# State-space branch: a quarter's circle computed behind the copy of the linear that ends next

## Chip, cores and metric

One core of one Trainium2 chip runs the whole program. The metric is the device time of one execution in microseconds (us); the kernel before takes 3046.33 us, the median of 3 runs (3044.68 to 3046.96).

## What is computed

Two transformer-like blocks on 512 tokens of width 1024, in float32. The change lies in the first block, in its state-space (S5) branch, which runs interleaved with the linears of the block's other branches:

```python
def first_block(x, ...):
    n = rms_norm(x, mix_norm_g)
    proj = n @ w_in
    xa, zu, zv = proj[..., :OFF_U], proj[..., OFF_U:OFF_V], proj[..., OFF_V:OFF_GA]
    gate_a, gate_b = sigmoid(...), sigmoid(...)
    ya = s5_branch(xa, ...)        # this one
    yb = sgu_branch(zu, zv, ...)
    ...

def s5_scan(u, lam_re, lam_im, log_step, b_re, b_im, c_re, c_im, reverse):
    lam_bar = exp(lam * step)
    b_bar = ((lam_bar - 1.0) / lam)[..., None] * b
    bu = einsum('gpc,lbgc->lbgp', b_bar, u)
    _, states = associative_scan(_linear_recurrence, (a, bu), axis=0, reverse=reverse)
    return einsum('gcp,lbgp->lbgc', c, states).real
```

The states are complex. The kernel takes 8 tokens as one chunk, so that 64 chunks are scanned, and rotates the inputs of the scan by the angle of each chunk, scans real and imaginary parts with a real decay, and rotates back. The cosines and sines of these angles are "the circle".

## The kernel before

Every linear is cut into units of 128 rows of its weight matrix (8 units for most linears). For each unit SyncE loads the weights into one of 8 slots, ScalarE rounds them to `wH` (`round_units`, L1321, an ACTIVATE Copy of 128x512), GpSimd subtracts to get the rest `wL` (L2874), and TensorE does 12 matmuls (L726: three passes over four blocks). `wH` and `wL` have four buffers, so ScalarE rounds a unit once the unit four before it has been used up.

PSUM is two halves of four banks. Half 0 takes the linears of this stretch (`azv0`, `azv1`, `azu0`, `azu1`, `aga0`, `agb0`), half 1 takes the small jobs of the state-space branch. When a linear ends, `linear_read` (on ScalarE, L1334) reads its four banks one by one with Gelu or Sigmoid; the next linear's first unit writes bank by bank behind it. A job of half 1 waits, in `fill`, until the job before it in the half has been read (`drained[1]`).

The order is written out by hand in `S5_STEPS`, a list of (task, quarter, units of the linears done before it), which TensorE and ScalarE both follow. The branch runs in four quarters. Those steps that matter, with the units: `("taps", 1, 14), ("turn_y", 0, 16), ("drive", 1, 17)`, then `("taps", 2, 23), ("turn_y", 1, 24), ("drive", 2, 25)` and `("taps", 3, 31), ("turn_y", 2, 32), ("drive", 3, 33)`. So on TensorE the order is: taps of quarter q (L866), one or two units, `turn_y` of quarter q-1 (32 small transposes, L906), one unit, `drive` of quarter q (64 small matmuls, L880), further units. Units 15, 23 and 31 (counted from 0) are the last of `azv1`, `azu0` and `azu1`.

On ScalarE each step first rounds the units that are due (four ahead of TensorE), with `linear_read` ahead of the rounding that pairs with a linear's last unit, and then does the step's task: for `turn_y` the copy `turned_y` of the transposed outputs from half 1 (an ACTIVATE Copy, L1312, which also frees half 1), for `out` a Gelu from PSUM (L1312) and the rounding of the next quarter's angles (L1469), for `taps` of quarters 1 to 3 `circle(q)`: Abs (L1474), Sin (L1475) and Sin (L1476), each 128x512, the Abs and the first Sin each waited for by the next. Sin and Gelu need different activation tables, and the compiler puts an ACT_TABLE_LOAD where the table changes.

VectorE rounds off the angles (`fraction`, L2224), which `circle(q)` waits for, and its `scan(q)` (L2318 and on) waits for `drive(q)` and for the circle. `out(q)` on TensorE waits for the states of `scan(q)`.

Of the kernel before, what the change touches and what calls it, by code (L numbers as in the profile page):

```python
# [57 lines left out]
SPLITS = 4  # L58
# [248 lines left out]
def two_blocks(nc, I, out):  # L307
    ring, jobs = Ring(), Jobs()
    ds = bass.ds
    with ExitStack() as ctx:  # L310
# [161 lines left out]

        forward = [[(0, 512, 0, 0)], [(1, 384, 512, 512), (3, 128, 896, 896)], [(2, 256, 1024, 1024)]]
        ret_at = {j: to for bank in forward for j, _, _, to in bank}

        def done(eng, name, l=0, i=0):
# [19 lines left out]
        def read_out(eng, name, l=0, i=0):  # L496

            eng.wait_ge(drained[jobs.half[name]], jobs.nth(name, l, i) + 1)
# [808 lines left out]
        def _(act):  # L1307
            link = Chain(act, S["act_step"])
            act.dma_start(consts[:, 0:2 * P], I["consts"][:, 0:2 * P]).then_inc(S["consts_loaded"], 16)
            def evac(dst, src, h, func=ACT.Copy, **kw):  # L1310

                act.activation(dst, src, func, **kw).then_inc(drained[h], 1)  # L1312

            def round_units(name, l, i, units, cols):
                for u in units:
                    s, p = ring.slot[(name, u)], ring.split[(name, u)]
                    act.wait_ge(landed[s], ring.at(ring.landed, name, u, l, i))
                    free = ring.at(ring.before, name, u, l, i) + ring.split_room[(name, u)]
                    if free > 0:
                        act.wait_ge(weights_used, free)  # L1320
                    act.activation(wH[:, p, 0:cols], slot[:, s, 0:cols], ACT.Copy).then_inc(weights_high, 1)  # L1321
# [135 lines left out]
            def plain_x(g):  # L1457

                act.wait_ge(S["plain_turned"], g + 1)
                h = jobs.half["aplain1" if g else "ahx0"]  # L1460
                evac(hT[:, 4 * g:4 * g + 4, :], banks(h), h)
# [4 lines left out]
            def angles_whole(q):  # L1466

                act.wait_ge(S["s5_angles"], 2 * q + 1)
                act.activation(decays_k, rot_cos, ACT.Identity, bias=rounder).then_inc(S["s5_circles"], 1)  # L1469

            def circle(q):

                act.wait_ge(S["s5_angles"], 2 * q + 2)
                link(act.activation(decays_k, rot_sin, ACT.Abs))  # L1474
                link(act.activation(rot_sin, rot_sin, ACT.Sin, scale=-TWO_PI))  # L1475
                act.activation(rot_cos, decays_k, ACT.Sin, bias=half_pi, scale=-TWO_PI).then_inc(S["s5_circles"], 1)  # L1476
# [8 lines left out]
            def turned_y(q):  # L1485

                act.wait_ge(S["s5_y_turned"], q + 1)
                evac(y[:, q, :].rearrange("p (k s) -> p s k", s=8), ps[1][:, 0:T].rearrange("p (s k) -> p s k", s=8), 1)

            def linear_read(name):  # L1490

                done(act, name)
                h = jobs.half[name]
                if name == "azv0":
                    act.wait_ge(S["x_moved"], 16)
                if name[:3] == "azv":
                    at = 512 * int(name[3])
                    evac_by_bank(zv[:, :, at:at + 512], h, ACT.Gelu_apprx_tanh)
                elif name[:3] == "azu":
                    at = 4 * int(name[3])  # L1500
                    evac_by_bank(zu[:, at:at + 4, :], h, ACT.Gelu_apprx_tanh)
                else:
                    evac_by_bank(gates_a[name[1:]], h, ACT.Sigmoid)

            ahead_units = S5_UNITS + [("aglu", u) for u in range(4)]
            rounded = SPLITS
            for task, q, units in S5_STEPS:
                for (name, u), (used, of_it) in zip(ahead_units[rounded:units + SPLITS], S5_UNITS[rounded - SPLITS:units]):
                    if of_it == KD - 1:
                        linear_read(used)  # L1510
                    round_units(name, 0, 0, [u], 512)
                rounded = units + SPLITS
                if task == "plain":
                    plain_x(q)
                elif task == "turn_u":
                    act.wait_ge(S["s5_u_turned"], 1)
                    evac(ush, ps[1][:, :].rearrange("p (g k) -> p g k", k=CHUNKS), 1)
                elif task == "turn_v":
                    act.wait_ge(S["s5_v_turned"], q + 1)
                    evac(VT, ps[1][:, :].rearrange("p (n e s) -> p n e s", n=2, e=8), 1)  # L1520
                elif task == "taps" and q:
                    circle(q)
                elif task == "out":
                    act.wait_ge(S["s5_out"], q + 1)
                    evac(yk.rearrange("p s (j c) -> p j s c", j=4), ps[1][:, 0:T].rearrange("p (j s c) -> p j s c", j=4, s=8), 1,
                         ACT.Gelu_apprx_tanh)
                    if q < QUARTERS - 1:
                        angles_whole(q + 1)
                    if q == 2:
                        act.dma_start(wsn, I["sgu_w"].rearrange("h t s -> t h s")).then_inc(S["sgu_w_loaded"], 16)  # L1530
                    elif q == 3:
                        act.dma_start(lng, I["sgu_ln_g"].unsqueeze(0).to_broadcast([P, D])).then_inc(S["sgu_loaded"], 16)
                        act.dma_start(lnb, I["sgu_ln_b"].unsqueeze(0).to_broadcast([P, D])).then_inc(S["sgu_loaded"], 16)
                        act.dma_start(sgub, I["sgu_bias"].unsqueeze(0).to_broadcast([P, H, P])).then_inc(S["sgu_loaded"], 16)
                elif task == "turn_y":
                    turned_y(q)
                    if q == 2:
                        read_out(act, "aturn_y2")
                        act.activation(yH[:, 0:3, :], y[:, 0:3, :], ACT.Copy).then_inc(S["ya_high"], 1)
                    elif q == 3:  # L1540
                        read_out(act, "aturn_y3")
                        act.activation(yH[:, 3, :], y[:, 3, :], ACT.Copy).then_inc(S["ya_high"], 1)
                if task == "drive" and q == 3:
                    act.wait_ge(S["zv_moments"], 1)
                    act.activation(stat[:, 56:60], stat[:, 48:56].rearrange("p (a b) -> p a b", b=2)[:, :, 1], ACT.Sqrt, bias=eps)\
                       .then_inc(S["zv_moments"], 1)
# [1426 lines left out]
```

## Time and profile before

| what | value |
|---|---|
| median of 3 runs | 3046.33 us |
| the profiled execution: time | 3046.19 us |
| the profiled execution: span, first to last instruction | 3044.4 us |
| TensorE busy | 3000.9 us, 99% of the span |
| ScalarE busy | 1279.4 us, 42% |
| VectorE busy | 1377.9 us, 45% |
| GpSimd busy | 1390.1 us, 46% |
| mean granted TensorE clock | 0.997 |

The profile is of one execution. A line names an engine (PE is TensorE, DVE VectorE, ACT ScalarE, POOL GpSimd), the line of the kernel, the operation and its tiles. Instructions of an engine overlap at their ends, so the time between two starts, not the duration, is what a further one adds. TensorE's granted clock is 1.00 at 2.4 GHz and 0.50 at 1.2 GHz.

### The profile page before, as it was taken

What the parts mean: (1) busy time and instruction counts of PE and PEld (TensorE: products, weight loads), DVE (VectorE), ACT (ScalarE), POOL (GpSimd) and SP (SyncE); (2) the same over time, 40 slices, a digit from 0 to 9 for tenths busy, and PEclk for the clock granted to TensorE, in tenths of its full rate; (3) what the DMA queues carried; (4) which work ended last, traced back from release to release, by engine and by line L of the source; (5) the groups of instructions that cost most, each with busy time, mean ns of one, the idle gap of its engine ahead of it and who ended that gap; (6) DMA issues with size and microseconds to landing.
All of it is one profiled execution on the core that took longest, in us unless ns stands there. A gap on an engine that the chain in (4) does not pass through costs nothing.

```text
span 3044.4 us, 39864 instructions
## 1 busy us (share of the span) xinstructions
PE 3000.9 (99%) x15302; PEld 2426.5 (80%) x15302; DVE 1377.9 (45%) x2171; ACT 1279.4 (42%) x2203; POOL 1390.1 (46%) x1002
## 2 busy tenths in 40 slices
PE   8999999999999999999999999999999999999998
PEld 7778887788888777778888888878777788878887
DVE  7874351421114877562116433167866520264322
ACT  5443343433333445454234443244454433354432
POOL 6335574444444542134455454554322354544543
PEclk9999999999999999999999999999999999999999
DMA  5334242233333422123333333244231133333332
GB/s 158 85 110 144 87 135 87 80 97 97 99 96 92 135 76 81 49 67 87 97 92 99 94 97 98 84 111 136 71 86 41 61 101 97 97 91 97 97 97 72
DMA packets 214891, 287.61 MB, mean 94 GB/s; under 512 B 42682, under 2 KB 122610, under 8 KB 213042
## 3 DMA queue, kind: packets, MB, share of 16 engines
q1 hardware_dynamic: 212210, 279.88, 31.5%
q0 software_dynamic: 880, 2.99, 0.3%
q8 instruction: 121, 1.98, 0.3%
q10 hardware_dynamic: 1616, 2.23, 0.2%
q14 instruction: 64, 0.52, 0.1%
HBM read 269.80 MB, written 4.72 MB: 90 GB/s over the span
## 4 chain that ended last, share of the span: by engine, by line
PE 91%; DVE 4%; ACT 2%; POOL 1%; issue 1%; DMA 0%; SPq 0%; ACTq 0%; DVEq 0%
PE half L726 81%; PE half L1125 2%; PE half L1156 2%; PE half L1142 2%; PE half L1211 1%; POOL wL L2874 1%; DVE arena L2052 1%; PE half L981 0%; PE half L998 0%; DVE rms L2043 0%; PE half L1197 0%; PE half L896 0%; DVE nL L2059 0%; ACT arena L1334 0%; DMA slot<-in_w_in 0%
## 5 line engine op out<-in xcount | busy, mean ns | idle before, releaser
L2874 POOL TENSOR_TENSOR wL<-slot,wH 128x512 fp32r<-128x512 f32 (+1 forms) x976 | 1358.4, 1399 | 1624.8 <-ACT wH L1321 1623.7
L1321 ACT ACTIVATE wH<-slot 128x512 fp32r<-128x512 f32 (+1 forms) x976 | 603.7, 625 | 1228.7 <-PE half L726 1223.5
L726 PE MATMUL half<-nH,wH 128*128 128x512 f32 x2336 | 924.1, 396 | 8.8 <-POOL wL L2874 3.2
L726 PE MATMUL half<-nH,wL 128*128 128x512 f32 x2336 | 910.5, 390 | 0.0
L726 PE MATMUL half<-nL,wH 128*128 128x512 f32 x2336 | 909.4, 389 | 0.0
L726 PE MATMUL half<-arena_split,wH 128*128 128x512 f32 (+1 forms) x2432 | 735.8, 385 | 2.6 <-ACT arena L1334 1.4
L726 PEld LDWEIGHTS half<-nH,wH 128*128 128x128 f32 x2336 | 438.4, 188 | 118.6 <-issue 18.1
L726 PEld LDWEIGHTS half<-arena_split,wH 128*128 128x128 f32 x2432 | 451.1, 188 | 95.4 <-issue 4.2
L726 PEld LDWEIGHTS half<-nH,wL 128*128 128x128 f32 x2336 | 438.5, 188 | 92.4
L726 PEld LDWEIGHTS half<-nL,wH 128*128 128x128 f32 x2336 | 438.8, 188 | 89.3 <-issue 1.4
L726 PE MATMUL half<-arena_split,wL 128*128 128x512 f32 (+1 forms) x1216 | 466.4, 384 | 0.0
L726 PEld LDWEIGHTS half<-arena_split,wL 128*128 128x128 f32 x1216 | 228.5, 188 | 45.2
L2790 DVE TENSOR_TENSOR arena<-half,arena 128x2048 f32<-128x2048 f32 x16 | 36.7, 2292 | 322.6 <-PE half L726 306.8
L2822 DVE SCALAR_TENSOR_TENSOR arena<-half,vec,arena 128x511 f32<-128x511 f32 (+1 forms) x160 | 108.8, 743 | 159.7 <-ACT arena L1984 159.0
L1833 ACT ACTIVATE arena<-half 128x512 f32<-128x512 f32 (+2 forms) x128 | 68.5, 535 | 230.5 <-PE half L1142 230.5
L2073 DVE TENSOR_TENSOR arena_split<-arena,arena_split 128x1024 fp32r<-128x1024 f32 (+3 forms) x44 | 69.1, 1570 | 149.5 <-ACT arena_split L1689 114.3
L726 PE MATMUL half<-wH,nH 128*128 128x512 f32 (+1 forms) x288 | 110.3, 383 | 5.7 <-DVE nL L2059 3.4
L2677 DVE TENSOR_SCALAR arena<-arena,small 128x512 f32<-128x512 f32 (+2 forms) x192 | 110.8, 619 | 3.4
L726 PE MATMUL half<-wH,nL 128*128 128x512 f32 (+1 forms) x288 | 106.9, 371 | 0.0
L726 PE MATMUL half<-wL,nH 128*128 128x512 f32 (+1 forms) x288 | 106.6, 370 | 0.0
L2085 DVE TENSOR_TENSOR hT<-hT,half 128x2048 f32<-128x2048 f32 x7 | 16.0, 2287 | 193.5 <-PE half L726 193.5
L1820 ACT ACTIVATE arena<-arena,small 128x512 f32<-128x512 f32 (+2 forms) x192 | 100.9, 533 | 6.3 <-DVE small L2690 6.3
(349 smaller groups left out, 2651.0 us busy)
## 6 DMA issues: line engine op xcount, KB each, us to landing
slot<-in_w_in SPq DMA_DIRECT2D x344, 256.0 KB, 2.7
slot<-in_w_up SPq DMA_DIRECT2D x440, 128.0 KB, 2.1
slot<-in_w_down SPq DMA_DIRECT2D x132, 256.0 KB, 2.7
slot<-in_w_branch SPq DMA_DIRECT2D x64, 256.0 KB, 2.7
slot<-in_w_out SPq DMA_DIRECT2D x48, 256.0 KB, 2.9
slot<-in_w_gate SPq DMA_DIRECT2D x88, 128.0 KB, 2.1
arena<-arena SPq DMA_DIRECT2D x40, 256.0 KB, 4.4
slot<-in_w_proj_b SPq DMA_DIRECT2D x16, 256.0 KB, 2.9
```

The costliest lines, as they stand in the source:

```text
L726: mm = pe.matmul(dst, lhsT, rhs, start=(k == 0 and m == 0), stop=(k == last and m == 2))
L1125: mm = pe.matmul(half[:, S_AT[p]:S_AT[p] + n], queries[br][HD * p:HD * p + HD, i, b * P:b * P + P], keys_at(br, i, p, k0, n), start=True, ...
L1142: mm = pe.transpose(half[:, at:at + P], logits(s, p)[:, k:k + P], ident)
L1156: mm = pe.matmul(half[HD * p:HD * p + HD, O_AT + b * P:O_AT + b * P + P], values_at(br, i, p, (k0 + k) // P), probs_turned(s)[:, p * n + k ...
L1321: act.activation(wH[:, p, 0:cols], slot[:, s, 0:cols], ACT.Copy).then_inc(weights_high, 1)
L1820: ins = act.activation(logits(s, p), logits(s, p), ACT.Exp, bias=nm[:, p:p + 1], accum_out=total[:, p:p + 1])
L1833: act.activation(probs_turned(s)[:, to:to + wide_n], half[:, T_AT:T_AT + wide_n], ACT.Copy)\
L2073: return dve.tensor_tensor(part, whole_value, plainly(high), ALU.subtract)
L2677: ins = dve.tensor_scalar(logits(s, p), logits(s, p), inv[:, p:p + 1], None, ALU.mult)
L2790: link(dve.tensor_tensor(gate if n else sums, banks(h), gate, ALU.mult))
L2822: ins = dve.scalar_tensor_tensor(out=conv[:, p, j, shift:T], in0=src[:, j * T:j * T + T - shift], scalar=vec[:, ds(ch + at, 1)], in1=conv[ ...
L2874: pool.tensor_tensor(wL[:, p, 0:cols], slot[:, s, 0:cols], plainly(wH[:, p, 0:cols]), ALU.subtract)\
```

## The change

`circle(q)` for the quarters 1 to 3 is no longer issued in the step `taps`. The step only remembers the quarter, and the next step (`turn_y` of quarter q-1) issues the circle behind its rounding of units and the `linear_read` among them, and ahead of its own task. The circle of quarter 0 stands elsewhere and stays. No instruction of another engine moves.

```diff
             ahead_units = S5_UNITS + [("aglu", u) for u in range(4)]
-            rounded = SPLITS
+            rounded, circle_of = SPLITS, None
             for task, q, units in S5_STEPS:
                 for (name, u), (used, of_it) in zip(ahead_units[rounded:units + SPLITS], S5_UNITS[rounded - SPLITS:units]):
                     if of_it == KD - 1:
                         linear_read(used)
                     round_units(name, 0, 0, [u], 512)
                 rounded = units + SPLITS
+                if circle_of:
+                    circle(circle_of)
+                    circle_of = None
                 if task == "plain":
                     plain_x(q)
...
                 elif task == "taps" and q:
-                    circle(q)
+                    circle_of = q
```

The order on ScalarE around the second quarter (unit numbers from 0), before: round 26, circle(2), `linear_read("azu0")`, round 27, `turned_y(1)`. After: round 26, `linear_read("azu0")`, round 27, circle(2), `turned_y(1)`.

## Rows read from the trace of the kernel before

**Rows 1.** The page's part 1: busy time, share of the span, instructions.
```profile
PE 3000.9 (99%) x15302; PEld 2426.5 (80%) x15302; DVE 1377.9 (45%) x2171; ACT 1279.4 (42%) x2203; POOL 1390.1 (46%) x1002
```
**Rows 2.** Waits of TensorE, us 60 to 300: who, for what, us in total, times, longest.
```profile
PE half L726 <- ACT arena L1334: 1.6, 2, 0.8
```
**Rows 3.** ScalarE in order of time, second quarter: start us, duration us, line, op.
```profile
140.99 0.60 ACT L1312 ACTIVATE arena<-half 128x512 f32<-128x512 f32 x1 [4.88 <-PE half L896]
...
144.01 0.63 ACT L1321 ACTIVATE wH<-slot 128x512 fp32r<-128x512 f32 x1 [1.80 <-PE half L726]
144.63 0.63 ACT L1474 ACTIVATE arena<-arena 128x512 f32<-128x512 f32 x1
145.28 1.28 ACT L1475 ACT_TABLE_LOAD   x1
146.57 0.63 ACT L1475 ACTIVATE arena<-arena 128x512 f32<-128x512 f32 x1
147.24 0.72 ACT L1476 ACTIVATE arena<-arena,small 128x512 f32<-128x512 f32 x1
147.98 1.28 ACT L1334 ACT_TABLE_LOAD   x1
149.27 2.07 ACT L1334 ACTIVATE arena<-half 128x512 f32<-128x512 f32 x4
151.20 0.65 ACT L1321 ACTIVATE wH<-slot 128x512 fp32r<-128x512 f32 x1
151.72 1.21 ACT L1312 ACTIVATE arena<-half 128x512 f32<-128x512 f32 x1
```
**Rows 4.** TensorE in order of time, second quarter, then third; idle before in brackets.
```profile
148.04 1.15 PE L906 MATMUL half<-consts,arena 64*64 64x64 f32 x32
150.01 0.47 PE L726 MATMUL half<-nH,wH 128*128 128x512 f32 x1 [0.82 <-ACT arena L1334]
...
152.98 2.09 PE L880 MATMUL half<-arena 128*64 128x64 f32 x64
...
183.32 1.15 PE L906 MATMUL half<-consts,arena 64*64 64x64 f32 x32
185.29 0.47 PE L726 MATMUL half<-nH,wH 128*128 128x512 f32 x1 [0.83 <-ACT arena L1334]
...
188.26 2.09 PE L880 MATMUL half<-arena 128*64 128x64 f32 x64
```
**Rows 5.** ScalarE in order of time, first quarter moved.
```profile
113.79 2.07 ACT L1334 ACTIVATE hT<-half 128x512 f32<-128x512 f32 x4 [0.72 <-PE half L726]
115.72 0.65 ACT L1321 ACTIVATE wH<-slot 128x512 fp32r<-128x512 f32 x1
116.24 1.20 ACT L1312 ACTIVATE arena<-half 128x512 f32<-128x512 f32 x1
```
**Rows 6.** TensorE in order of time, first quarter moved.
```profile
113.68 1.15 PE L906 MATMUL half<-consts,arena 64*64 64x64 f32 x32
114.76 0.50 PE L726 MATMUL half<-nH,wH 128*128 128x512 f32 x1
...
117.71 2.09 PE L880 MATMUL half<-arena 128*64 128x64 f32 x64
```
**Rows 7.** VectorE in order of time, first quarter moved: the scan's first instruction.
```profile
119.84 0.69 DVE L2318 TENSOR_TENSOR arena<-half,arena 128x512 f32<-128x512 f32 x1 [2.87 <-PE half L880]
```
**Rows 8.** ScalarE, us 212 to 216: a table load and the activation behind it.
```profile
212.26 1.28 ACT L1312 ACT_TABLE_LOAD   x1
215.23 0.60 ACT L1312 ACTIVATE arena<-half 128x512 f32<-128x512 f32 x1 [1.69 <-PE half L896]
```
**Rows 9.** TensorE in order of time: the transposes of L801, and two other stalls.
```profile
39.42 1.91 PE L801 MATMUL half<-consts,arena 128*128 128x128 f32 x16
...
51.13 3.29 PE L801 MATMUL half<-consts,arena 128*128 128x128 f32 x16 [2.88 <-ACT arena L1312]
...
978.86 0.48 PE L726 MATMUL half<-wH,nH 128*128 128x204 f32 x1 [1.69 <-DVE nL L2059]
...
1684.21 0.50 PE L726 MATMUL half<-nH,wH 128*128 128x512 f32 x1 [1.57 <-POOL wL L2874]
```
**Rows 10.** Busy time in stretches; then granted clock, DMA share, GB/s.
```profile
50.00:51.00 1.00, 0.00 (x0) 0.00 (x0) 1.00 (x1) 1.00 (x2) 1.00 (x2) 0.74 0.00 0
51.00:52.00 1.00, 0.87 (x4) 0.87 (x5) 1.00 (x2) 0.59 (x2) 1.00 (x1) 0.50 0.00 0
...
53.00:54.00 1.00, 1.00 (x7) 1.00 (x6) 1.00 (x2) 0.00 (x0) 0.96 (x1) 0.56 0.00 0
...
979.00:980.00 1.00, 1.00 (x6) 1.00 (x6) 1.00 (x3) 0.59 (x1) 0.00 (x0) 0.50 0.67 147
...
1682.00:1690.00 8.00, 6.43 (x28) 4.99 (x27) 6.51 (x9) 3.43 (x6) 5.03 (x4) 1.00 0.42 126
```

## Prediction

> **What bounds the kernel now.** I read the page's busy times first: TensorE is busy 99% of the span and the three other engines under half [rows 1]. So a change on ScalarE is worth only what it does to TensorE's idle time, and the next view is who TensorE waits for in the stretch of the change. From us 60 to 300 there is one entry: two waits, 1.6 us together, for `linear_read` [rows 2]. The third view, both engines in order of time, shows why. In the second quarter ScalarE does circle(2) from 144.63 to 147.96, then a table load to bring Gelu back (1.28 us), and reads the first bank only at 149.27 [rows 3]; TensorE began `turn_y` behind the last unit at 148.04 and stands still 0.82 us ahead of the next linear's first unit [rows 4]. The third quarter has the same pattern with 0.83 us [rows 4]. In the first of the moved quarters nothing is late: the Gelus start at 113.79, after 0.72 us of waiting for TensorE [rows 5], and TensorE goes on at 114.76 without idle time [rows 6].
>
> **What the change removes.** With the circle behind `linear_read`, the Gelus of quarters 2 and 3 start when the last unit ends. In the first quarter that is 0.11 us after the start of `turn_y` (113.79 against 113.68) [rows 5, 6], so 148.15 and 183.43 in the other two. The table is still Gelu's there, since the last ScalarE work with a table of its own was the Gelu of `out` at 140.99 [rows 3]. TensorE then goes on 1.08 us after `turn_y` began, as it does in the first quarter (114.76 - 113.68) [rows 6]: at 149.12 and 184.40. Gain 0.89 us in each of two quarters, 1.8 us in all, and none in the first.
>
> **What it moves, and who stands behind it.** The circle doesn't vanish: it goes in front of `turned_y`. That copy frees half 1 of PSUM, and `drive(q)`, one unit behind `turn_y` on TensorE, waits for exactly that in `fill`. The cover there is one unit. In the first quarter `turned_y` runs from 116.24 to 117.44 [rows 5], and `drive` starts at 117.71, or 117.78 when the matmul before it is counted to its end [rows 6]: 0.3 us to spare. In the second, `turned_y` ends at 152.93 and `drive` starts at 152.98 [rows 3, 4]: nothing to spare.
>
> The circle's length is one row minus another: from the start of Abs, 144.63, to the end of the second Sin, 147.96: 3.33 us, with its table load of 1.28 us inside [rows 3]. That the load remains where it stands follows from Gelu being active before it and Sin needed in it. I take the full 3.33 us as the shift of `turned_y`; if the copy can begin 0.1 us before the Sin ends, as neighbours without a dependence do (the rounding from 151.20 takes 0.65, the next copy starts at 151.72) [rows 3], the shift is 3.2.
>
> - First quarter: `turned_y` at 116.24 + 3.33 = 119.57, ends 1.20 later at 120.77; a release of TensorE by ScalarE takes 0.1 (149.27 + 0.61 for one of four Gelus gives 149.88, next matmul 150.01 [rows 3, 4]). `drive` at 120.87 instead of 117.78: **+3.1 us**. All of it is new idle time of TensorE.
> - Second quarter: Gelus 148.15, round +1.93 = 150.08, Abs +0.52 = 150.60 (distances of the starts in rows 3), `turned_y` at 153.93, ends 155.14, `drive` at 155.24 instead of 153.02: **+2.2 us**. TensorE's unit ends at about 152.1, so it idles 3.1 us here too; the 0.89 us gained are already inside the 2.2.
> - Third quarter: the same distances (183.43 for 148.15), 190.52 instead of 188.30: **+2.2 us**.
>
> Sum of the waits: +7.5 us (three idle times of 3.1, less 1.8 gained); with the shorter shift of 3.2 it is 7.2.
>
> **The rest of the moved step.** Rounding of weights behind `turned_y` comes some 3 us later, but four units are prepared and TensorE itself stands still for as long; I cost it at nothing, and it would cost only if a unit were needed within that time. The scan waits for `drive` and the circle. Now the scan starts when `drive` ends (119.84) [rows 7]; then the circle is done at 119.57 and `drive` later than before, so the circle ends earlier than needed: nothing. The circle's own wait for VectorE's fraction is long met: nothing. The circle issues no DMA and no queue of SyncE or GpSimd is passed. Gelu's table must be loaded again before the next `out`: a load stands ahead of the wait of its activation, as at 212.26 with the Gelu at 215.23 [rows 8], and ahead of `out` ScalarE idles 4.88 us [rows 3]: nothing; without that cover 1.28 us each.
>
> **The clock.** Each of the three new stalls is about 3 us long. After a stall of 2.88 us the granted clock went to 0.50, that is 1.2 GHz, and was back at 2.4 GHz only inside the stretch 53 to 54; the 16 transposes behind it took 3.29 us, against 1.91 at full clock [rows 9, 10]: 1.4 us lost. After a stall of 1.69 us it fell too (0.50 from 979), after one of 1.57 us it didn't [rows 9, 10]. The new stalls are nearer to 2.88 than to either, so I take 1.4 us for each: **+4.2 us**. Bounds: 0, if the clock is kept, and 1.7 each when the whole time at half clock falls on work: 0.74 is the mean of a stretch with 0.52 us of it at 0.50, 0.56 of one with 0.88 us, and two whole stretches lie between, 3.4 us together [rows 10]; 5.1 in all. A gain is excluded, the clock being at its upper level already.
>
> **Against the skill.** The table load in the circle runs from 145.28 to 146.56 and the Sin starts at 146.57 [rows 3]: a switch costs 1.28 us, with nothing behind it. The Trainium skill, page "ScalarE: Activation LUTs", section "What ACT_TABLE_LOAD costs", gives 1283 ns for the load, which this trace bears out, and 1380 ns of drain on top for each switch, which it doesn't. By the page's whole price an estimate would put 1.4 us more before each of the three `turned_y`, and the time at 3062.2 us.
>
> **Sum.** 3046.19 (the profiled execution: a span of 3044.4 and 1.8 around it) + 7.5 + 4.2 = 3057.9; it lies 0.14 under the median of the runs, so against the median 3046.33 + 11.7 = **3058.0 us**. Downstream nothing should take this back: what follows on all engines is released by TensorE's own progress, and TensorE is busy 99%.
>
> **Rivals.**
> 1. *The stalls come, the clock stays.* Speaks for it: a stall of 1.57 us left it at 1.00. Against: 1.69 and 2.88 didn't. Time 3046.3 + 7.5 = 3053.8. Chance 0.13.
> 2. *The clock falls behind one or two of the stalls only*, or where it costs less: 3055.2 to 3056.6. Chance 0.22.
> 3. *Not slower: the unit between `turn_y` and `drive` covers the circle.* Only the two late Gelus go: 3046.3 - 1.8 = 3044.5, no difference that can be measured. It decides at the point where Abs, load and two Sins fit in what is spare ahead of `drive`, 0.3 us in the first quarter and none in the second; they take 3.33 us. It could hold only if `drive` didn't wait for `turned_y`, and `fill` says it does. Chance 0.03.
> 4. *The change doesn't reorder as I read it*, for example the compiler drops or adds table loads: one load fewer within each circle makes the waits 3 x 1.28 us shorter, 3.7 us instead of 7.5, and the stalls, 1.8 us, sit at the edge of the clock's fall: 3050.0 to 3054. Chance 0.05.
> 5. *A switch costs the page's 2.66 us when Sin follows Gelu and copies*: 3062.2. The three switches of the trace speak against it; chance 0.01.
>
> The forecast itself, 3057 to 3059.5, has 0.56.
>
> **How the numbers follow.** The likeliest is 3058.0. The range takes in rival 1 and most of rival 2 below, and 1.7 us per clock fall plus about 1 us for the runs' own spread above: 3053.0 to 3060.5. What a measurement of this kernel can tell from no change is 0.2%, 6.1 us, that is 3052.4. Forecast and rivals 1, 2 and 5 lie above it (0.92), and half of rival 4 too: slower 0.94, same 0.05, faster 0.01.
>
> **What would show it.** In the profile after: `linear_read` of quarters 2 and 3 without a table load ahead and 0.1 us after `turn_y` begins, and no wait of TensorE for L1334; three new waits of L880 for ScalarE's L1312, about 3.0 us each; granted clock 0.50 for a few us at each; VectorE's scan still released by L880. Wrong would be: `drive` starting less than 1 us after its unit, circles before the Gelus, or the added time found elsewhere than from us 114 to 195.

## The result, and the profile after

| | us |
|---|---|
| before, median of 11 runs | 3046.81 (3044.68 to 3047.57) |
| changed, median of 11 runs | 3054.96 (3051.67 to 3059.18) |
| ratio, 95% interval | 1.0028 (1.0020 to 1.0036) |
| changed, profiled execution | 3059.18, span 3057.4 |

The change makes the kernel 8.15 us slower, 0.28%. The prediction had +11.7 us. The profiled execution happens to be the slowest of the eleven, and this matters below.

TensorE's waits from us 60 to 270 in the changed kernel (who for whom, us in total, times, longest):

```profile
PE half L880 <- ACT arena L1312: 8.5, 3, 2.8
```

The two waits for `linear_read` [rows 2] are gone; three waits of `drive` for `turned_y` have come, 2.83 us each. ScalarE in order of time, second quarter (start us, duration us):

```profile
151.24 0.64 ACT L1321 ACTIVATE wH<-slot 128x512 fp32r<-128x512 f32 x1 [1.80 <-PE half L726]
155.17 2.07 ACT L1334 ACTIVATE arena<-half 128x512 f32<-128x512 f32 x4 [3.30 <-PE half L726]
157.10 0.65 ACT L1321 ACTIVATE wH<-slot 128x512 fp32r<-128x512 f32 x1
157.62 0.65 ACT L1474 ACTIVATE arena<-arena 128x512 f32<-128x512 f32 x1
158.29 1.28 ACT L1475 ACT_TABLE_LOAD   x1
159.59 0.63 ACT L1475 ACTIVATE arena<-arena 128x512 f32<-128x512 f32 x1
160.25 0.72 ACT L1476 ACTIVATE arena<-arena,small 128x512 f32<-128x512 f32 x1
160.88 1.07 ACT L1312 ACTIVATE arena<-half 128x512 f32<-128x512 f32 x1
```

This answers [rows 3]: the Gelus (L1334) have no table load ahead of them, and `turned_y` (L1312) comes only behind the Sin. TensorE, the same quarter:

```profile
155.07 1.15 PE L906 MATMUL half<-consts,arena 64*64 64x64 f32 x32
...
162.00 3.31 PE L880 MATMUL half<-arena 128*64 128x64 f32 x62 [2.83 <-ACT arena L1312]
```

`turn_y` begins at 155.07, the Gelus 0.10 us later, and `drive` stands still for 2.83 us, to be compared with [rows 4]. It also runs slowly: 3.31 us for the 62 of its matmuls that the trace holds, where [rows 4] has 2.09 for 64. The granted clock of the stretches at the three drives (the third number from the end) says why:

```profile
121.00:122.00 1.00, 0.00 (x0) 0.00 (x0) 0.00 (x0) 1.00 (x3) 0.00 (x0) 0.70 0.66 225
122.00:123.00 1.00, 0.76 (x14) 0.76 (x16) 0.00 (x0) 0.62 (x2) 0.30 (x1) 0.50 0.00 0
...
125.00:126.00 1.00, 1.00 (x19) 0.88 (x15) 0.03 (x1) 0.00 (x0) 0.00 (x0) 0.50 0.78 221
...
128.00:129.00 1.00, 1.00 (x5) 0.78 (x5) 1.00 (x3) 0.00 (x0) 0.00 (x0) 0.89 0.00 0
...
162.00:163.00 1.00, 1.00 (x24) 1.00 (x26) 0.00 (x0) 0.37 (x1) 0.55 (x1) 0.68 0.32 121
...
165.00:166.00 1.00, 1.00 (x10) 0.84 (x9) 0.54 (x1) 0.00 (x0) 0.00 (x0) 0.62 0.61 205
...
200.00:201.00 1.00, 0.40 (x8) 0.40 (x10) 0.00 (x0) 0.97 (x2) 0.00 (x0) 0.50 0.98 367
...
203.00:204.00 1.00, 1.00 (x26) 0.93 (x24) 0.05 (x1) 0.99 (x2) 0.93 (x1) 0.84 0.00 0
```

The three falls are not alike: at the first drive the clock is at 1.2 GHz for 6.8 us, at the second and the third for 3.4 us each. VectorE's scan is still released by `drive`, as predicted (DVE, us 100 to 260):

```profile
DVE arena L2321 <- PE half L880: 17.7, 3, 7.4
```

**A measure free of the start.** The first 50 us of the kernel differ by a us or more between executions, so I compare one stage: from the first `turn_v` (first row of L854) to the transposes behind the branch (L936). Before:

```profile
63.86 1.91 PE L854 MATMUL half<-consts,arena 128*128 128x128 f32 x16
...
238.48 0.71 PE L936 MATMUL half<-consts,arena 128*128 128x128 f32 x5
```

174.6 us before. In the changed kernel's profile the same rows start at 65.52 and 252.01: 186.5 us, 11.9 more. Three waits of 2.83 less two gains of 0.89 are 6.7; the other 5.2 lie where the clock is at 1.2 GHz. What follows the stage takes 2805.3 to 2806.2 us in every profile of this document (2805.9 before, 2805.4 in this one), so nothing behind it takes the loss back.

### The profile page after: what moved, and what is told of

It is laid out like the page before. It is cut to its first block, busy times and chain, and to the rows that moved or that the text cites. A ratio compares the mean times of both kernels' runs of the same rounds, so it can differ in the third digit from the quotient of the medians.

```text
span 3057.4 us, 39863 instructions
## 1 busy us (share of the span) xinstructions
PE 3004.5 (98%) x15302; PEld 2429.7 (79%) x15302; DVE 1378.1 (45%) x2171; ACT 1277.4 (42%) x2202; POOL 1394.7 (46%) x1002
## 4 chain that ended last, share of the span: by engine, by line
PE 90%; DVE 4%; ACT 2%; POOL 1%; issue 1%; DMA 0%; SPq 0%; ACTq 0%; DVEq 0%
PE half L726 80%; PE half L1125 2%; PE half L1156 2%; PE half L1142 2%; PE half L1211 1%; POOL wL L2877 1%; DVE arena L2055 1%; PE half L981 0%; PE half L998 0%; ACT arena L1334 0%; DVE rms L2046 0%; PE half L1197 0%; PE half L880 0%; PE half L896 0%; DVE nL L2062 0%
```

## The experiments

Each was timed beside the kernel before on the same chip, on three occasions, each with a chip of its own; the kernel before had medians of 3046.0 to 3046.6 us there. The stage's length comes from each one's own profile, of one execution; the 174.6 us of the kernel before are from one execution too.

| kernel | median us (before beside it) | stage us | against 174.6 |
|---|---|---|---|
| change, first profile | 3054.96 (3046.81) | 186.5 | +11.9 |
| change again | 3053.69 (3046.59) | 181.4 | +6.8 |
| change, third profile | 3053.61, one run (3046.52) | 181.5 | +6.9 |
| only circle(1) moved | 3049.72 (3046.04) | 177.5 | +2.8 |
| only circles 2 and 3 moved | 3049.89 (3046.04) | 178.5 | +3.9 |
| no table load in the circles | 3049.97 (3046.04) | 177.6 | +3.0 |
| circle behind turned_y | 3046.82 (3046.04) | 174.6 | 0.0 |
| the same, Abs early | 3045.65 (3046.59) | 173.8 | -0.8 |
| Sins ahead of turned_y, Abs early | 3053.91 (3046.52) | 181.5 | +6.8 |
| two copies more | 3064.90 (3046.59) | 191.9 | +17.3 |
| drive one unit later | 3048.71 (3046.59) | 176.7 | +2.1 |
| each quarter in its own place | 3044.60 (3046.52) | 173.3 | -1.4 |

### Taking the change apart

My theory: the loss is `drive` waiting for `turned_y`, once per moved circle. The rivals: it belongs to ScalarE's order as a whole, or the quarters take it up from each other.

```diff
                 elif task == "taps" and q:
-                    circle_of = q
+                    if q == 1:
+                        circle_of = q
+                    else:
+                        circle(q)
```

> Only circle(1) is moved behind linear_read, circles 2 and 3 stay where they were before. Theory of the stall in front of drive: one wait of 2.83 us, nothing gained, 3046.8 + 2.8 = 3049.6 us with the clock kept and 3051.0 us with 1.4 us for a fall of the clock; the two waits of 0.8 us in quarters 2 and 3 are still there. Rival, that the loss belongs to the late quarters or to the whole order of ScalarE: 3046.8 us.

Waits of TensorE in this kernel, us 60 to 270:

```profile
PE half L880 <- ACT arena L1312: 2.8, 1, 2.8
PE half L726 <- ACT arena L1334: 1.6, 2, 0.8
```

One new wait, both old ones still there, stage +2.83 us, time +3.7 us (interval of the ratio 1.0004 to 1.0022). The counterpart, with `q == 1` doing its circle at once and the others remembered:

> circle(1) stays where it was before, circles 2 and 3 are moved. Two waits of 2.83 us less two gains of 0.89 us: +3.9, so 3050.7 us with the clock kept and 3053.5 us with 1.4 us for each of two falls. If the parts add, this and the kernel with only circle(1) moved make up the whole change: their two differences to before sum to its 8.2 us. Rival, that one quarter's delay is taken up by the next: the sum would be clearly above or below 8.2.

Two waits of 2.83, none for L1334, stage +3.89 us, time +3.85. The stage's two differences sum to 6.72, which is what the whole change shows in the profiles of it without a fall of the clock in the stage (6.8 and 6.9). The differences of the two medians sum to 7.5 us, between the 7.1 and 8.15 of the whole change. Nothing is taken up by a later quarter: the parts add, and the rival falls.

### The table load in the circle

```diff
-                link(act.activation(rot_sin, rot_sin, ACT.Sin, scale=-TWO_PI))
-                act.activation(rot_cos, decays_k, ACT.Sin, bias=half_pi, scale=-TWO_PI)...
+                turn = ACT.Identity if q else ACT.Sin
+                link(act.activation(rot_sin, rot_sin, turn, scale=-TWO_PI))
+                act.activation(rot_cos, decays_k, turn, bias=half_pi, scale=-TWO_PI)...
```

> The whole change, with the two Sins of circles 1 to 3 replaced by Identity of the same sizes, so that no table is loaded (the rotation is then wrong from quarter 1 on). It takes 1.28 us out of each stall in front of drive: waits of about 1.55 us instead of 2.83, three of them, less two gains of 0.89: 3046.8 + 2.9 = 3049.7 us if the clock stays up behind stalls of this length, as it did behind those of 1.57 us in the trace before; with falls as behind stalls of 2.83 it would be 3051 to 3054 us. If table switches had the 1.4 us of drain on top that does not show in the trace, the waits would be 0.2 us.

This kernel leaves out the sines of circles 1 to 3, and with them the table loads.

Waits of TensorE in this kernel, us 60 to 270:

```profile
PE half L880 <- ACT arena L1312: 4.7, 3, 1.6
```

Waits of 1.55 to 1.58 us, so the load is worth 1.28 us in each and no more, and no drain stands behind it. The stage is 3.0 us longer, as computed (3 x 1.55 less 1.8), and the clock stayed at 1.00 around all three (busy time by engine in three stretches, clock the third number from the end):

```profile
118.00:128.00 10.00, 8.45 (x93) 6.93 (x92) 5.41 (x9) 3.68 (x6) 4.20 (x3) 1.00 0.37 113
154.00:164.00 10.00, 8.42 (x92) 6.93 (x92) 8.10 (x10) 3.63 (x6) 4.68 (x3) 1.00 0.46 127
190.00:200.00 10.00, 8.45 (x92) 6.92 (x92) 6.39 (x14) 6.77 (x9) 3.56 (x3) 1.00 0.44 125
```

### The same kernel twice more

> The changed kernel once more, unaltered, beside the others on the same chip. Waits of 2.83 us in front of the three drives again. Theory: whether the clock falls behind such a stall differs from execution to execution, so the time spreads over several us (3051.7 to 3059.2 in its first 11 runs, where the kernel before spreads over 3 us); the profiled execution should show fewer than three falls or shorter ones, and its stage from the first turn_v to the transposes behind the branch be 174.6 + 6.7 us plus half of the time at half clock. Rival, the falls belong to the stalls as surely as in its first profile: three falls and 186.5 us again.

The stretches around its three stalls (busy time of TensorE is the second number, granted clock the third from the end):

```profile
118.00:128.00 10.00, 7.17 (x87) 5.98 (x86) 4.61 (x8) 4.11 (x6) 2.95 (x3) 1.00 0.27 82
155.00:165.00 10.00, 7.17 (x87) 5.90 (x86) 6.86 (x10) 4.35 (x6) 3.45 (x3) 1.00 0.43 120
193.00:203.00 10.00, 7.35 (x87) 6.37 (x88) 5.18 (x9) 6.77 (x9) 2.81 (x2) 1.00 0.37 112
```

The same three stalls of 2.83 us, and no fall behind any. The stage is 181.4 us, which is 174.6 + 6.8: the waits and nothing else. Its median is 7.1 us over before, its runs lie between 3052.9 and 3056.4; those of the kernel before lie between 3043.6 and 3048.1 on that occasion.

> The changed kernel unaltered, one more profiled execution. Its first profile had three falls of the clock behind three stalls of 2.83 us, its second none. Theory, a fall differs from execution to execution: any number from 0 to 3, and the stage from the first turn_v to the transposes behind the branch is 181.4 us plus half of the working time at half clock. Rival, that the first profile's falls were of one chip or one bad run: none, 181.4 us.

None again, 181.5 us. The only fall in this profile up to the end of the stage lies at us 51 to 54, behind the stall that [rows 9] shows there before as well. So the number of falls varies from one profiled execution to another. These three were on different occasions, so by themselves they don't show that the chip plays no part. But the runs of one occasion differ in the clock too: the four slowest of the first eleven (3055.6 us and above) are the four whose mean granted clock is 0.996 or less, and so are the three slowest of the eight on the second occasion (3055.6 and above). Of the stalls of 2.83 us in the profiles of the change and of its two halves, 3 of 12 were followed by a fall, all three in one execution.

### Longer stalls

```diff
                 link(act.activation(decays_k, rot_sin, ACT.Abs))
+                if q:
+                    link(act.activation(decays_k, decays_k, ACT.Copy))
+                    link(act.activation(decays_k, decays_k, ACT.Copy))
```

> The whole change with two more copies of 128x512 in each of circles 1 to 3, about 0.67 us each one waiting for the other. Theory: each adds to the wait of drive one to one, waits of about 4.15 us instead of 2.83, so 4.0 us more than the change, plus what the clock costs. The clock: if a stall of 2.83 us pulls it down in some executions and in others not, one of over 4 us should in all: three falls costing 1.4 to 1.7 us each, time 3046.5 + 6.7 + 4.0 + 4.6 = 3061.8. If the clock were as indifferent to the length as between 2.83 and 2.87, and costs 0.5 us per stall on average: 3058.7.

Waits of TensorE, us 60 to 270, and then the stretches around the three stalls:

```profile
PE half L880 <- ACT arena L1312: 12.5, 3, 4.2
```
```profile
119.00:129.00 10.00, 6.23 (x73) 5.66 (x74) 2.50 (x5) 4.08 (x6) 1.27 (x1) 0.66 0.20 56
159.00:169.00 10.00, 5.84 (x71) 5.18 (x71) 4.01 (x5) 4.63 (x6) 2.25 (x2) 0.66 0.38 114
200.00:210.00 10.00, 5.97 (x71) 5.40 (x72) 2.36 (x6) 7.50 (x9) 1.28 (x1) 0.66 0.37 112
```

Each added copy went one to one into the wait (4.16 us for 2.83), and all three stalls brought the clock down, for 6.8 us each (0.34 of 10 us below full, doubled). At us 51 it was some 3.4, in the change's first profile once 6.8 and twice 3.4. The change itself was profiled on the same chip (the second profile) and had no fall behind its stalls of 2.83 us. The time is 3064.9, 18.3 us over before and 3 us over my expectation: 10.7 are waits, and in the stage's 17.3 us the clock has the other 6.6, or 2.2 per stall.

### Shorter stalls

Abs stays in the old place, load and Sins go ahead of `turned_y`:

```diff
+            def circle_size(q):
+                act.wait_ge(S["s5_angles"], 2 * q + 2)
+                link(act.activation(decays_k, rot_sin, ACT.Abs))
...
                 elif task == "taps" and q:
+                    circle_size(q)
                     circle_of = q
```

> The whole change with the Abs of circles 1 to 3 left in the old place; table load and both Sins stay ahead of turned_y. Theory: the wait of drive is the length of what stands ahead of turned_y less the cover; the Abs adds 0.67 us to it, but a table load can't begin before the copy ahead of it has ended, where Abs could, so 0.67 less 0.1 is saved: three waits of about 2.25 us, stage 174.6 + 3 x 2.25 - 1.8 = 179.6 us without falls of the clock. For the clock: its stalls lie between those of 1.55 us, which never pulled it down, and those of 2.83 us, which did in some executions; if each profiled stall is a draw, 0 to 2 of three fall here, the time 3051.5 to 3054.

Waits of 2.31, 2.39 and 2.37 us, about 0.1 more than expected. One of them had a fall behind it (clock 0.57 over us 193 to 197), stage 181.5 instead of 179.9. The time, 3053.9, is no better than that of the change, though the waits are 1.4 us less in all; the two kernels ran on different occasions, and with falls that come and go their medians don't separate such a difference.

### Behind turned_y

```diff
                 elif task == "turn_y":
                     turned_y(q)
+                    if circle_of:
+                        circle(circle_of)
+                        circle_of = None
```

The call of `circle` ahead of the tasks is removed.

> The circle is issued one place later still: behind linear_read and also behind turned_y. If the time of the change is lost in front of drive(q), because turned_y frees half 1 late, both the 0.9 us gained in quarters 2 and 3 stay and the three waits of 2.83 us go: 3046.8 - 1.8 = 3045.0 us, no wait of TensorE for L1312, clock 1.00 in us 100 to 200. The circle then ends about 1 us after drive, so VectorE's scan starts about 1 us late in each quarter; its slack ahead of out(q) is 1.9 us (135.39 - 133.49 in the trace before), so this costs nothing. Rival: the circle is simply too late for the scan wherever it stands behind linear_read, and out(q) waits for the states: three times about 1 us more, 3048 us or above. Second rival, the loss is not in front of drive at all: about 3055 us.

Waits of TensorE, us 60 to 270:

```profile
PE half L866 <- DVE arena L2298: 1.6, 2, 0.8
PE half L891 <- issue: 0.4, 2, 0.2
```

No wait of `drive` any more, none for L1334: the loss of the change is gone, and with it the rival that it lay elsewhere. But the gain isn't there either. Two waits of `taps` (L866) have come in its place, 0.78 and 0.79 us. They are for VectorE's outputs matrix, the matrix that `taps` and `out` multiply by; the stage is as long as before, and the time 0.8 us over before within an interval of 0.9994 to 1.0012. VectorE in order of time (the scan's first instruction and the end of the outputs matrix) shows the way:

```profile
119.71 0.69 DVE L2321 TENSOR_TENSOR arena<-half,arena 128x512 f32<-128x512 f32 x1 [3.65 <-ACT arena L1476]
...
142.64 1.34 DVE L2298 SCALAR_TENSOR_TENSOR arena<-arena 128x1152 f32<-128x1152 f32 x1
```

The scan is now released by the second Sin (L1476) and no longer by `drive`. It starts 2.92 us behind the start of `drive` (116.79), where [rows 6, 7] have 2.13: 0.8 us late. I had counted the slack ahead of `out`, 1.9 us, and that held nearly (0.2 us each). The outputs matrix of the next quarter stands behind the scan in VectorE's queue, and `taps` waits for it without slack.

### Abs early, and each quarter in its own place

First the circle behind `turned_y` with the Abs of circles 1 to 3 left in the old place:

> As the kernel with the circle behind turned_y, but its Abs (which needs no table of its own) stays where the whole circle stood before, and only the table load and the two Sins come behind turned_y. Theory: behind turned_y the whole circle made VectorE's scan start 0.9 us after drive's end, which came out again as a wait of 0.8 us of taps(2) and taps(3) for the outputs matrix. With the Abs away the scan starts 0.68 us earlier, so those waits shrink from 0.79 to about 0.1 us, and the waits for linear_read stay gone: from the first turn_v to the transposes behind the branch 173.3 us instead of 174.6 before, that is 1.3 to 1.4 us less than before. Time about 1.4 us below before, 3044.7, which only the stage and not the median can show. Rival, the 0.8 us are a cost of the freed Gelus themselves (the linear restarting sooner) and not of the late scan: the waits of 0.79 us stay and the stage takes 174.6.

The waits of `taps` are 0.63 and 0.71 us, not 0.1; the stage 173.8 instead of 173.3. From ScalarE in order of time in this kernel:

```profile
116.58 1.19 ACT L1312 ACTIVATE arena<-half 128x512 f32<-128x512 f32 x1
117.78 1.28 ACT L1480 ACT_TABLE_LOAD   x1
119.08 0.63 ACT L1480 ACTIVATE arena<-arena 128x512 f32<-128x512 f32 x1
```

The table load starts at the end of the copy ahead of it (116.58 + 1.19). In the kernel of the section ahead, Abs started 0.94 us behind the start of that copy, overlapping its end. So taking Abs away saved 0.4 us, not 0.7, and the scan is still 0.4 us late. My arithmetic was off. The time, 3045.65 us against 3046.59, isn't to be told from before (0.9988 to 1.0006). The rival, that the 0.8 us have nothing to do with the scan, falls too, since `taps(2)` came 26.84 us behind `drive(1)` here, 27.25 in the kernel ahead and 26.34 before [rows 6] (144.05 - 117.71).

Then, against the kernel just described:

```diff
                 elif task == "taps" and q:
-                    circle_size(q)
-                    circle_of = q
+                    if q < 3:
+                        circle_size(q)
+                    if q == 1:
+                        circle(q)
+                    else:
+                        circle_of = q
```

Circle 3 does its Abs with its Sins, behind `turned_y(2)`.

> Each quarter's circle where the runs so far say it costs least. Circle(1) stays where it was before, since nothing waited for it there. Circle(2): Abs in the old place, Sins behind turned_y(1). Circle(3): whole, behind turned_y(2), since no taps come behind scan(3). Theory: linear_read is 0.89 us earlier in quarters 2 and 3, taps(2) isn't late, taps(3) by 0.5 us as in the kernel with the Abs early, out(3) not at all, because seven units stand ahead of it: the stage from the first turn_v to the transposes behind the branch takes 174.6 - 1.8 + 0.5 = 173.3 us, the time is 1.3 us under before (about 3045.3), which the medians can hardly show. Rival, out(3) or the split of its outputs is late after all by the 0.9 us of the scan: 174.2.

Waits of TensorE, us 60 to 270:

```profile
PE half L866 <- DVE arena L2310: 0.7, 1, 0.7
```

One wait left, which puts `taps(3)` 26.91 us behind `drive(2)` where it was 26.34 before; stage 173.3 us as computed, 1.4 under before. The median is 3044.60 against 3046.52, but the interval of the ratio is 0.9985 to 1.0003: faster than before in the stage of its profile, and in whole runs not to be told from it. Against the change it is 9 to 10 us less.

### The cover of drive

```diff
-            ("out", 0, 13), ("taps", 1, 14), ("turn_y", 0, 16), ("drive", 1, 17), ...
+            ("out", 0, 13), ("taps", 1, 14), ("turn_y", 0, 16), ("drive", 1, 18), ...
```

and the same for 25 and 33.

> The whole change, with drive(1), drive(2) and drive(3) one unit later on TensorE (behind two units, not one, after turn_y). Theory of the cover: a unit of 2.7 us more lies between turn_y and drive, and the wait of drive for turned_y falls from 2.83 to about 0.1 us. But VectorE is as late as in the change: drive ends 2.8 us later than before, the scan as well, the outputs matrix and with it taps(2) and taps(3), which had 0.1 us to spare, so these wait 2 to 2.8 us instead. Time within 1.5 us of the change without its clock losses, about 3052. Rival, VectorE has slack enough (1.9 us ahead of out): only small waits, and the gain of the Gelus stays: 3045 to 3047.

Waits of TensorE, us 60 to 270:

```profile
PE half L891 <- issue: 1.8, 2, 0.9
PE half L866 <- DVE arena L2298: 1.6, 2, 0.8
PE half L880 <- ACT arena L1312: 0.5, 3, 0.2
```

The waits of `drive` are 0.5 us in all: the cover is what they are made of. Those of VectorE's late chain take their place, in front of `out` (L891) and `taps` (L866), 3.4 us together. I expected 2 to 2.8 each for `taps`; it is 1.7 per quarter with that of `out`. VectorE began the scan 9.11 us behind `turn_y`, 6.16 before [rows 6, 7]; but from the scan's first instruction to the end of the outputs matrix it took 23.1 us there and 24.2 in the profile before (its four scans alone 3.34 and 4.45), and 1.1 us of the lateness was gone. Such single instructions of VectorE that take 1.1 us more, in one execution here and in another there, stand in every profile; their cause stays open. The time is 3048.71 us, where I expected about 3052 and the rival had 3045 to 3047: it lies between them, and its interval, 0.9997 to 1.0015, doesn't separate it from before.

## Why the prediction was right, step by step

- **Which waits go, which come, and their place**: as predicted, in each quarter. The Gelus start 0.10 us after `turn_y`, no table load ahead. `out`'s load is hidden.
- **The sum of the waits**: 7.5 predicted, 6.7 measured. The mis-sized term is the new idle time, 2.83 us and not 3.1 in each quarter. I had let `turned_y` begin when the Sin ended, and last 1.20; it began 0.63 us after the Sin's start (160.88 against 160.25), that is 0.09 before the Sin's end, lasted 1.07, and `drive` followed 0.05 after it and not 0.1: 0.27 us in all. My lower bound, 7.2, was still too long.
- **The clock**: that it can fall at such a stall was right, that it falls at each was not. I predicted one fall of 1.4 us behind each stall, 4.2 in all, from one row of a stall of nearly the same length [rows 9, 10]. One execution had three falls, two had none. The step that failed is that one execution's row says what a stall does, where it says only what it can do: the stall of [rows 9] itself, 2.86 to 2.88 us at us 51, had no fall behind it in four of the thirteen profiles (circle behind turned_y, circles 2 and 3 moved, drive later, Sins ahead of turned_y).
- **The cost of a fall**: from one `drive` to the next, and from the last to the end of the stage, the first profile took 2.5, 1.3 and 1.2 us more than the second, whose clock stayed up. So 1.4 was near for the two falls of 3.4 us; the one of 6.8 us cost more than my bound of 1.7 for each. Together they are 5.1 us (5.2 against the profile before), at my bound for all three.
- **The length of a stall as a measure**: I took 1.4 us for each because 2.83 is nearer to 2.88 than to 1.69 or 1.57. The thirteen profiles don't bear out that order. The stalls of 1.68 and 1.69 us at some us 979 and 2020 were followed by a fall in 18 of 26 cases, those of 2.83 us in 3 of 12.
- **The time**: 3058.0 against 3054.96, or +11.7 against +8.15. It is inside 3053.0 to 3060.5 and outside the 3057 to 3059.5 to which I gave 0.56. It lies between rival 1 (the clock stays, 3053.8) and rival 2 (one or two falls, 3055.2 to 3056.6). With the measured waits of 6.7 us, rival 1 would be 3053.5. The interval of the ratio, 6.1 to 11.0 us over before, doesn't tell these apart, and of the three profiled executions two show rival 1, one the forecast's three falls and none rival 2. In the medians the falls would have 1.4 and 0.4 us left (8.15 and 7.1 less 6.7), neither clear of noise. I gave rival 1 too little; the median lies inside the range because the range was opened downward for it, and not because the clock did what I forecast.
- **Rival 3**, that the unit covers the circle: it didn't hold. The kernel with `drive` one unit later shows how much cover it would have taken, and that VectorE then is the next bound.
- **Downstream takes nothing back**: right. The stage of the second profile is 6.8 us longer and the runs' median 7.1, what follows the stage is as long as before, and the parts add up.
- **"The circle is earlier than needed for the scan"**: right for the change, only because `drive` was late as well. Without that, behind `turned_y`, it is 0.8 us late.
- **The table switch**: 1.28 us, nothing behind it; taking it out shortened the waits by 1.28 us (2.83 to 1.55). The estimate with 1.4 us of drain is refuted here, where the load stands in a chain that TensorE waits for.

## What to carry to other kernels

Moving a step on an in-order engine moves everything that stands behind it: list what it is moved in front of, and how much TensorE has in hand before it asks for that. Here 1.8 us less of waits were paid for with three times 2.83 us of new ones. When a chain has no slack at its old place (here the fraction, circle and scan of VectorE), the step can be late on both sides; look for the slack of each instance by itself, since the first, the middle and the last quarter differed.

## What the hardware showed that I had not expected

- The same stall can pull TensorE's clock to 1.2 GHz in one execution and leave it at 2.4 GHz in the next. In the stage, over all profiles: stalls of 1.55 to 1.58 us 0 of 3; 2.31 to 2.39 us 1 of 3; 2.83 us 3 of 12; 4.16 us 3 of 3. But the length alone doesn't decide it: the stall of 2.86 to 2.88 us at us 51 was followed by a fall in 9 of 13 profiles, with and without one on each of the three chips of the experiments; those of 1.68 to 1.69 us in 18 of 26, and those of 1.56 to 1.59 us at some us 1684 and 2725 in 0 of 26. What decides it for a given stall wasn't settled.
- A fall need not cost what it costs in the stage. From the stall at us 979 to the matmul behind a wait at us 1259 (L1142) the profile before, with a fall, took 280.3 us, and the three without one 279.7: 0.6 us. From the stall at us 2019 to L1142 it was 281.0 with a fall of 3.4 us and 281.0 without. Where the clock stays up, TensorE reaches the rest `wL` of the weights too early and waits for GpSimd instead, as in the kernel with each quarter in its own place (us 970 to 990):

```profile
PE half L726 <- DVE nL L2074: 1.7, 1, 1.7
PE half L726 <- POOL wL L2889: 0.8, 1, 0.8
```

- The changed kernel's slowest runs are those with the lowest mean granted clock. Whether its times scatter more than those of the kernel before isn't shown: 7.5 us from lowest to highest against 2.9 in the first eleven runs each, but 3.5 in eight against 4.5 in 24 on the second occasion, and the kernel before alone spread over 6.7 us in its 33 runs beside the first experiments.
- An ACT_TABLE_LOAD starts only at the end of the activation ahead of it (117.78, the copy ending at 117.77), where an independent activation starts 0.13 us [rows 3] to 0.23 us (Abs behind the copy in the kernel with the circle behind `turned_y`) earlier.
